# A two-block layer on one core: one group of experts per loop turn, the first expert routed on its own, and one-hot columns as weights in the first four gathers

## The chip, the cores and the metric

One core of one Trainium2 chip runs the whole kernel. The metric is the device time of one execution in microseconds. The kernel before was timed three times: 955.11, 957.72 and 958.09 us, median 957.72 us. The profile is of one further execution.

## The reference, cut to what matters

Two transformer-like blocks over 256 tokens of width 1024, all in float32. The first block is a hybrid mixer (Mamba-2 scan and a short convolution), then a hierarchical mixture of experts; the second block is another mixer and a dense feed-forward. The change touches the start of the kernel, the end of the first mixer and the experts. In the reference:

```python
h = h + hybrid_mixer(rmsnorm(h, norm_mix), ...)
hn = rmsnorm(h, norm_ffn)
h = h + hierarchical_moe(hn, ...)      # 4 groups of 8 experts
# of each token: the best group, the two best experts of that group,
# gates = softmax over groups at the best * softmax over the two logits
# expert e: (silu(x @ w_gate[e]) * (x @ w_up[e])) @ w_down[e]
```

Every expert's three matrices have 2 MB each (1024 x 512 floats), so the 32 experts bring 6 MB each.

## The kernel before, in words

**Memory.** The weights pass through `ring` (six slots of 2 MB), `pair_d` (two more) and three buffers for down matrices, `down_a`, `down_b`, `down_c`. `down_b` lies over `w_hi` and `w_lo`, the split halves of the weights of the first mixer, which are free once its last granule is multiplied. `res` holds the residual stream, 128 partitions (tokens) x 2 blocks x 1024.

**Start.** SP loads x into `x_tok` (L781). ACT and DVE square it, POOL forms the inverse root (`norm_pool`, L505), ACT scales block 1 (L487) and DVE block 0 (L500), PE transposes (`turn_pe`, L515). Meanwhile POOL copies x into `res` with the features reordered (`natural`, L912): in `res` the feature index 8p+c stands at place c*128+p, the order in which the experts' weights lie in memory.

**End of the first mixer.** The last granule of w_out leaves four PSUM banks. `add_res` (L677 to L684) adds them to `res` on DVE, in four pieces with reordered rows. PE transposes the sum for the router (L2200), ACT and DVE copy it out, PE forms the logits (L2209).

**Routing.** A chain of some forty small DVE operations (L1615 to L1675), each waiting for the one before, finds for each token its group and two experts. PE counts ranks (L2216 to L2219) once `member` says that the table of memberships is ready. Between them PE multiplies the identity by itself (`keep_running`, L2040: four and two times 512 columns), results unused. An expert has 32 slots a round; four experts make a group of 128 slots. `gather_first` (L2238) multiplies tokens (as weights, 128x128) by one-hot columns (32 or 96 moving) and so writes the gathered tokens already transposed; `keep_first` and `keep_rest` apply the gain.

**Experts.** `gate_up_apart` (L2251) is the first expert, whose gate matrix is read before its up matrix, so that the gate slot comes free early. `gate_up_pe` and `down_pe` are the others: the 32 gathered tokens are the weights, in four column tiles of the array, and the expert's matrix moves. `add_group` (L2301) scatters a group's results into four PSUM banks that add up over all groups. Groups 0 and 1 are written out; a hardware loop does two groups per turn, three turns here. At the end `add_last` adds the four banks to `res` on DVE (L1783) and PE transposes `res` for the second block (L2314).

**The queue of loads.** SP alone issues the loads of weights, in an order written out by hand (L820 to L868). At the start of the experts these are the last of expert 3 (`pair_d`), the down matrix of expert 1 (`down_b`, L837), then in two halves the gate matrix of expert 4, each behind a half of expert 0's gate product (`gate_read`, L802), then expert 4's up matrix behind expert 0's last product (`gu_raw` 1), expert 5's pair behind `gu_raw` 2, a down matrix behind `ye_raw` 1, and so on. A load behind a wait stops all that stand after it in this queue.

Of the kernel before, what the change touches and what calls it, by code (L numbers as in the profile page):

```python
# [85 lines left out]
def build(nc, ctx, x, w, out):  # L86
# [298 lines left out]
    moe_added = sem("moe_added")  # L385
# [344 lines left out]
    XT_BANK = 7  # L730
    TURN_BANK = ((0, 1, 2, 3, 5, 6, 7, 4), (0, 2, 4, 7, 1, 3, 5, 6), (4, 5, 6, 7, 0, 2, 1, 3))
# [48 lines left out]
    def _(sp):  # L780
        sp.dma_start(x_tok[:, :, :], x.rearrange("(b p) d -> p b d", p=P)).then_inc(ld_x, 16)  # L781
# [54 lines left out]
        load_half(3, 1, 3)  # L836
        load_down(1, 1)  # L837
# [31 lines left out]
        for u in range(UA, len(units)):  # L869
# [13 lines left out]
            if u == UA + SLOTS - 2:  # L883
                sp.wait_ge(const_ready, 6)
# [12 lines left out]
    def _(pool):  # L897
# [13 lines left out]
        for b in range(TB):  # L911
            nc.gpsimd.tensor_copy(natural(b), in_eights(x_tok[:, b, :]))  # L912
# [108 lines left out]
        pool.wait_ge(res_mix, 2)  # L1021
# [28 lines left out]
    def _(act):  # L1050
        load_rows(act, 0)
        act.wait_ge(ld_x, 16)
        norm_act(act, 0, x_tok, xdt)
# [21 lines left out]
        def keep_x(i):  # L1075
            if i == 0:
                act.wait_ge(const_ready, 2)
# [124 lines left out]
        nc.scalar.activation(y_e[:, :], res[:, 0, :], ACT.Square, accum_out=sm[:, 0:1]).then_inc(squared, 1)  # L1202
# [6 lines left out]
        nc.scalar.activation(y_e[:, :], res[:, 1, :], ACT.Square, accum_out=sm[:, 1:2]).then_inc(ss_act, 1)  # L1209
# [28 lines left out]
        group_act(1, 0)  # L1238
        act.wait_ge(routed, 1)
        n_more = act.value_load(rounds_i[0:1, 2:3], min_val=NE // 8 - 1, max_val=NE // 8 * (T // CAP) - 1)  # L1240
        with act.Fori(0, n_more) as i:
            for s in range(2):
                group_act(2 * i + (2 + s), 2 * i + (1 + s))
        keep_left(8 * n_more + 7, 3)

        hi(act, GA)
        hi(act, GA + 1)
# [153 lines left out]
    def _(dve):  # L1401
# [3 lines left out]
        norm_dve(dve, 0, x_tok, xdt)  # L1405
# [186 lines left out]

        def by_token(v, n):
# [19 lines left out]
        for b in range(TB):  # L1613
# [6 lines left out]
        nc.vector.tensor_reduce(g_top, by_group(G_LOGIT), AX_X, ALU.max)  # L1620
# [6 lines left out]
                                                     op0=ALU.mult, op1=ALU.add))  # L1627
        nc.vector.tensor_reduce(g_at, by_group(G_AT), AX_X, ALU.min)
# [26 lines left out]
        dve.wait_ge(rstd_ready, 2)  # L1655
# [877 lines left out]
```

## Time and profile before

| | us |
|---|---|
| three runs | 955.11, 957.72, 958.09 |
| profiled execution | 955.47 |
| its span | 953.7 |

The span is what the profile covers; 1.8 us of the profiled execution lie around it. Busy times and the span in 40 slices of 23.8 us, each digit a busy share in tenths:

```profile
PE 782.6 (82%) x6548; PEld 601.2 (63%) x6548; DVE 465.6 (49%) x815; ACT 318.0 (33%) x525; POOL 99.0 (10%) x116
PE   5999999999984764747646566479999999999997
DVE  6865849547421121201302012024968776766776
PEclk9999999999997887777979798779999999999999
DMA  9895243677999999999999999999975455555101
```

The first ten slices are the first mixer, slices 10 to 28 the experts, the rest the second block. PE leads on the sum, but a sum over stages is not a bound: in the experts' slices the DMA row stands at 9 and PE at 4 to 8, in the mixers it is the other way round. PEclk is the clock granted to TensorE in tenths of full speed.

### The profile page before, as it was taken

The numbers are of one execution on the slowest core, as the hardware profiler recorded it, in microseconds if no ns is written. First come the engines' busy times: TensorE is split into PE (matmuls) and PEld (weight loads), VectorE is DVE, ScalarE is ACT, GpSimd is POOL, SyncE is SP. The second block draws the span as 40 slices with busy tenths as digits, with TensorE's granted clock in tenths as the row PEclk, the third lists the DMA queues.
The fourth block names the chain that finished last, engine by engine and source line by source line (L and its number), as shares of the span: only waits on it lengthen the run. The fifth ranks groups of instructions, "written<-read, shape, count | busy, mean of one in ns | idle before, by whom it ended". The sixth has DMA issues, their size and how long they took to land.

```text
span 953.7 us, 15749 instructions
## 1 busy us (share of the span) xinstructions
PE 782.6 (82%) x6548; PEld 601.2 (63%) x6548; DVE 465.6 (49%) x815; ACT 318.0 (33%) x525; POOL 99.0 (10%) x116
## 2 busy tenths in 40 slices
PE   5999999999984764747646566479999999999997
PEld 5988999777643432334423333236888888888885
DVE  6865849547421121201302012024968776766776
ACT  5764346732100000000000000003597554444444
POOL 3019673300000000000000000000000100000000
PEclk9999999999997887777979798779999999999999
DMA  9895243677999999999999999999975455555101
GB/s 318 272 354 177 90 177 145 259 311 294 415 427 428 426 429 426 427 427 429 428 429 427 428 429 427 429 428 388 363 266 178 155 189 201 183 177 177 45 1 45
DMA packets 72534, 286.67 MB, mean 301 GB/s; under 512 B 11882, under 2 KB 38688, under 8 KB 59936
## 3 DMA queue, kind: packets, MB, share of 16 engines
q1 hardware_dynamic: 71876, 284.81, 75.9%
q10 hardware_dynamic: 604, 1.10, 0.3%
q8 instruction: 39, 0.64, 0.3%
q14 instruction: 15, 0.12, 0.0%
HBM read 284.85 MB, written 1.05 MB: 300 GB/s over the span
## 4 chain that ended last, share of the span: by engine, by line
PE 54%; DMA 28%; issue 8%; DVE 4%; POOL 3%; ACT 2%; SPq 1%; POOLq 0%; DVEq 0%; ACTq 0%
DMA pair_d<-in_w_up_dram 22%; PE bank L664 11%; PE bank L613 11%; PE bank L629 9%; PE bank L2264 5%; PE bank L626 4%; PE bank L2288 4%; PE bank L641 4%; DMA ring<-in_w_in_dram 3%; DMA down_b<-in_w_down_dram 3%; PE bank L2230 1%; PE bank L2238 1%; PE bank L2095 1%; POOL seg_r L946 1%; ACT w_hi L583 1%
## 5 line engine op out<-in xcount | busy, mean ns | idle before, releaser
L593 DVE TENSOR_TENSOR w_lo<-ring,w_hi 128x1024 fp32r<-128x1024 f32 x135 | 174.7, 1294 | 101.9 <-ACT w_hi L583 101.5
L583 ACT ACTIVATE w_hi<-ring 128x1024 fp32r<-128x1024 f32 x136 | 144.2, 1060 | 178.3 <-PE bank L629 64.1
L613 PE MATMUL bank<-act_p,w_hi 128*128 128x256 f32 x736 | 137.7, 288 | 3.1 <-issue 2.0
L1776 DVE COPY y_e<-bank 32x256 f32<-32x256 f32 x64 | 27.2, 424 | 222.5 <-PE bank L2288 222.1
L629 PE MATMUL bank<-act_p,w_hi 128*128 128x512 f32 x344 | 119.3, 397 | 0.0
L613 PEld LDWEIGHTS bank<-act_p,w_hi 128*128 128x128 f32 x736 | 115.3, 192 | 6.0 <-issue 3.9
L1226 ACT ACTIVATE y_e<-bank 32x256 f32<-32x256 f32 x64 | 23.9, 374 | 256.7 <-PE bank L2288 256.4
L613 PE MATMUL bank<-act_p,w_lo 128*128 128x256 f32 x368 | 104.3, 283 | 0.0
L2288 PE MATMUL bank<-down_b,h_t 128*32 128x256 f32 x480 | 40.3, 493 | 74.6 <-issue 64.1
L664 PE MATMUL bank<-w_hi,act_q 128*128 128x512 f32 x288 | 90.6, 396 | 1.4 <-issue 0.8
L2264 PE MATMUL bank<-ring,moe 128*32 128x256 f32 x1472 | 84.0, 380 | 7.1 <-DVE moe L1739 6.7
L626 PE MATMUL bank<-act_p,w_lo 128*128 128x256 f32 x344 | 89.5, 281 | 0.0
L2288 PEld LDWEIGHTS bank<-down_b,h_t 128*32 128x32 f32 x480 | 18.9, 136 | 91.6 <-issue 74.0
L2264 PEld LDWEIGHTS bank<-ring,moe 128*32 128x32 f32 x1472 | 46.9, 110 | 38.6 <-issue 8.6
L629 PEld LDWEIGHTS bank<-act_p,w_hi 128*128 128x128 f32 x344 | 62.5, 188 | 13.1 <-issue 1.2
L613 PEld LDWEIGHTS bank<-act_p,w_lo 128*128 128x128 f32 x368 | 70.7, 192 | 0.0
L2264 PE MATMUL bank<-pair_d,moe 128*32 128x256 f32 x512 | 43.6, 515 | 30.4 <-DMA pair_d<-in_w_up_dram 30.4
L626 PEld LDWEIGHTS bank<-act_p,w_lo 128*128 128x128 f32 x344 | 64.9, 189 | 3.4
L664 PEld LDWEIGHTS bank<-w_hi,act_q 128*128 128x128 f32 x288 | 52.5, 188 | 15.0 <-issue 1.7
L2288 PE MATMUL bank<-down_a,h_t 128*32 128x256 f32 x480 | 37.9, 468 | 25.6 <-DMA down_a<-in_w_down_dram 25.6
L664 PE MATMUL bank<-w_lo,act_q 128*128 128x512 f32 x144 | 56.3, 391 | 0.0
L2264 PEld LDWEIGHTS bank<-pair_d,moe 128*32 128x32 f32 x512 | 24.3, 146 | 49.5 <-issue 46.1
(409 smaller groups left out, 1058.5 us busy)
## 6 DMA issues: line engine op xcount, KB each, us to landing
ring<-in_w_up_dram SPq DMA_DIRECT2D x24, 2048.0 KB, 34.6
ring<-in_w_gate_dram SPq DMA_DIRECT2D x23, 2048.0 KB, 30.2
down_a<-in_w_down_dram SPq DMA_DIRECT2D x15, 2048.0 KB, 25.9
down_b<-in_w_down_dram SPq DMA_DIRECT2D x15, 2048.0 KB, 25.8
ring<-in_w_in_dram SPq DMA_DIRECT2D x14, 2048.0 KB, 17.4
ring<-in_w_ffn_in_dram SPq DMA_DIRECT2D x22, 1024.0 KB, 7.6
pair_d<-in_w_gate_dram SPq DMA_DIRECT2D x8, 2048.0 KB, 30.0
pair_d<-in_w_up_dram SPq DMA_DIRECT2D x8, 2048.0 KB, 34.4
```

The costliest lines, as they stand in the source:

```text
L583: nc.scalar.activation(parts(w_hi, g, view), view, ACT.Copy).then_inc(split_hi, 1)
L593: engine.tensor_tensor(parts(w_lo, g, view), view, h, ALU.subtract).then_inc(split_lo, 1)
L613: mm = nc.tensor.matmul(dst, parts(wt, g, grans[g][1])[:, k, :], a[:, x_part, k, :], start=(k == 0 and i == 0), stop=(k == KC - 1 and i == 2))
L626: mm = nc.tensor.matmul(dst[:, 0:T], parts(w_lo, g, grans[g][1])[:, k, :], a[:, 0, k, :], start=False, stop=False)
L629: mm = nc.tensor.matmul(dst[:, :], parts(w_hi, g, grans[g][1])[:, k, :], a[:, :, k, :], start=(k == 0), stop=(k == KC - 1))
L641: mm = nc.tensor.matmul(dsts[b], a[:, x_part, k0 + k, b * P:(b + 1) * P], parts(wt, g, grans[g][1])[:, k, :], start=(k0 + k == 0 and i == ...
L664: mm = nc.tensor.matmul(banks[2 * b + half][:, :], a_chunk[:, x_part, b * P:(b + 1) * P], wt[:, slot(g), half * 512:(half + 1) * 512], sta ...
L946: ins = nc.gpsimd.tensor_tensor(seg_r[:, n, :, :], bcast(m_le[:, :].unsqueeze(1), [P, 4, P]), bcast(adt_r[:, n, b, 4 * q:4 * q + 4].bitcas ...
L1226: ins = nc.scalar.activation(out_rows(e, j), down_rows(j), ACT.Copy)
L1776: ins = nc.vector.tensor_copy(out_rows(e, j), down_rows(j))
L2264: mm = nc.tensor.matmul(bank[GU_BANK[e % 2]][CAP * j:CAP * (j + 1), 0:2 * P], x_t[:, c, CAP * e:CAP * (e + 1)], gu[:, :, c, j * P:(j + 1) ...
L2288: mm = nc.tensor.matmul(bank[2][CAP * j:CAP * (j + 1), 0:256], h_t[:, e % 2, CAP * c:CAP * (c + 1)], dn[:, c, 256 * j:256 * (j + 1)], star ...
```

## The change

- **Start.** x is loaded straight into `res`, in its own feature order. POOL's two reordering copies (L911, L912) go.
- **End of the first mixer.** `add_res` writes the sum, in plain order, to a new place, `mixed(b)`, which lies in slot 0 of `w_hi` (block 0) and of `w_lo` (block 1), in the memory of `down_b`. PE's router transposes read `mixed` with a step of 8 floats. POOL copies `mixed` in the experts' order to `res` (two copies), and only then builds `m_lt`, the mask that the ranks need. SP's load of `down_b` waits for POOL's copies, the transposes and ACT's squares.
- **First expert alone.** Five small DVE operations decide from the logits whether a token goes to expert 0. Three matmuls with one column each give its rank, and expert 0's one-hot columns are made before the rest of the routing. The gather and the product of expert 0 run while DVE goes on; the full ranks follow on PE behind them.
- **First four gathers.** `gather_alone` takes the one-hot columns as weights (32 wide, in four column tiles) and moves 256 token values through each tile. Its result has slots in partitions, so DVE transposes it in 32x32 blocks and then applies the gain (`keep_alone`). Experts 1, 2 and 3 are gathered one at a time, expert 1 ahead of the others.
- **`keep_running`** multiplies 256 columns, not 512, and stands in other places and counts (3, 2, 2, 1, 6, 2).
- **Residual through PSUM.** In group 0 PE starts each of the four output banks with the identity times `res` (four products of 512 columns). At the end ACT and DVE copy two banks each to `res`; the four DVE adds go.
- **Loop.** Only group 0 is written out; the loop does one group per turn, seven turns.

```diff
+    def mixed(b):
+        at = (2 * b + slot(GA - 2)) * GR
+        return down_b[:, at:at + D]
@@ add_res
-            r = natural(b, 64 * half, 64 * half + 64)
+            cols = slice(half * 512, (half + 1) * 512)
             piece_ready(dve, n, at, g)
-            ins = nc.vector.tensor_tensor(r, r, in_eights(banks[2 * b + half][:, :]), ALU.add)
+            ins = nc.vector.tensor_tensor(mixed(b)[:, cols], res[:, b, cols], banks[2 * b + half][:, :], ALU.add)
@@ sync
-        sp.dma_start(x_tok[:, :, :], x.rearrange("(b p) d -> p b d", p=P)).then_inc(ld_x, 16)
+        sp.dma_start(res[:, :, :], x.rearrange("(b p) d -> p b d", p=P)).then_inc(ld_x, 16)
...
         load_half(3, 1, 3)
+        sp.wait_ge(const_ready, 4)
+        sp.wait_ge(tok_turned, 4)
+        sp.wait_ge(ss_act, 2)
         load_down(1, 1)
         load_first_gate()
@@ gpsimd
         norm_pool(pool, 0)
-        for b in range(TB):
-            nc.gpsimd.tensor_copy(natural(b), in_eights(x_tok[:, b, :]))
...
-        pool.wait_ge(res_mix, 2)
+        for b in range(TB):
+            pool.wait_ge(res_mix, b + 1)
+            ins = nc.gpsimd.tensor_copy(natural(b), in_eights(mixed(b)))
+        ins.then_inc(const_ready, 1)
@@ vector
+        def keep_alone(e):
+            dve.wait_ge(xt_raw, e + 1)
...
+            link_dve(dve, nc.vector.transpose(turned_rows, bank[ALONE_BANK[e]][:, 0:2 * P]))
+            nc.vector.tensor_tensor(x_t[:, :, CAP * e:CAP * (e + 1)], turned_rows.rearrange("p (c s) -> p c s", c=KC),
+                                    bcast(g_ffn[:, :].unsqueeze(2), [P, KC, CAP]), ALU.mult).then_inc(xt_kept, 1)
...
+        nc.vector.tensor_tensor(r8[:, 1, :, :], own, bcast(own[:, :, 0:1], [P, TB, EPG]), ALU.is_gt)
+        link_dve(dve, nc.vector.tensor_reduce(g_top, by_group(G_LOGIT), AX_X, ALU.max))
+        nc.vector.tensor_tensor(r8[:, 2, :, 1], by_group(G_LOGIT)[:, :, 0], g_top, ALU.is_ge)
+        link_dve(dve, nc.vector.tensor_reduce(r8[:, 2, :, 0], r8[:, 1, :, :], AX_X, ALU.add))
+        nc.vector.scalar_tensor_tensor(out=first, ..., op0=ALU.is_le, op1=ALU.mult).then_inc(member, 1)
+        ...                        # rank of expert 0, its one-hot columns: member 2
+        keep_alone(0)              # between two links of the chain
@@ build_group, start
-                keep_first(1)
                 gates()
+                keep_alone(1)
                 rounds()
+                keep_alone(2)
+                keep_alone(3)
                 gate_weights()
@@ tensor
-                                         res[:, b, c * P:(c + 1) * P], ident[:, :])
+                                         in_eights(mixed(b))[:, :, c], ident[:, :])
...
+        nc.tensor.matmul(bank[4][:, 0:1], m_lt[:, :], first[:, 0, :], start=True, stop=True)
+        nc.tensor.matmul(bank[4][:, 1:2], ones[:, :], first[:, 0, :], start=True, stop=False)
+        nc.tensor.matmul(bank[4][:, 1:2], m_lt[:, :], first[:, 1, :], start=False, stop=True).then_inc(rank_raw, 1)
+        keep_running(2)
...
+        def gather_alone(e, which, o):
+            for b in range(TB):
+                row = res[:, b, :].rearrange("t (c p) -> t c p", c=KC)
+                for j in range(4):
+                    mm = nc.tensor.matmul(bank[ALONE_BANK[e]][CAP * j:CAP * (j + 1), 0:2 * P],
+                                          onehot[:, which, b, o:o + CAP], row[:, :, CAP * j:CAP * (j + 1)],
+                                          start=(b == 0), stop=(b == TB - 1))
+            mm.then_inc(xt_raw, 1)
@@ group_pe, before is None
+                gather_alone(0, 1, 0)
+                keep_running(2)
                 gate_up_apart(0)
+                keep_running(1)
+                ranks()
+                keep_running(6)
                 pe.wait_ge(built, 2)
-                gather_first(CAP, P - CAP, bank[5:7], 0)
+                gather_alone(1, 0, CAP)
+                keep_running(2)
+                pe.wait_ge(xt_kept, 2)
+                gate_up_pe(k, 1)
+                for e in range(2, 4):
+                    gather_alone(e, 0, CAP * e)
...
         group_pe(0, None)
-        group_pe(1, 0)
...
-            for s in range(2):
-                group_pe(2 * i + (2 + s), 2 * i + (1 + s))
+            group_pe(i + 1, i)
```

## Rows read from the trace of the kernel before

**Rows 1.** The chain that ended last, in order of time: start us, us, what.
```profile
549.21 34.41 DMA pair_d<-in_w_up_dram
...
636.60 26.40 DMA ring<-in_w_in_dram
```

**Rows 2.** Stretches of the span: busy per engine, then PEclk, DMA share, GB/s.
```profile
229.50:230.00 0.50, 0.50 (x4) 0.26 (x2) 0.34 (x2) 0.00 (x0) 0.00 (x0) 1.00 0.16 66
...
233.00:260.00 27.00, 26.57 (x477) 19.31 (x477) 14.57 (x54) 5.21 (x15) 0.00 (x0) 1.00 0.91 363
260.00:640.00 380.00, 238.14 (x2835) 135.51 (x2834) 74.45 (x204) 27.21 (x80) 0.00 (x0) 0.82 1.01 428
```

**Rows 3.** SP's issues in order of time: start us, us of issuing, engine, line, transfer.
```profile
216.54 0.43 SPq L808 DMA_DIRECT2D down_b<-in_w_down_dram  x1
...
234.65 1.20 SPq L803 DMA_DIRECT2D ring<-in_w_gate_dram  x2
237.26 0.33 SPq L795 DMA_DIRECT2D ring<-in_w_up_dram  x1
...
268.37 0.35 SPq L795 DMA_DIRECT2D ring<-in_w_gate_dram  x1
```

**Rows 4.** The first microseconds in order of time; the last is line L1860's query.
```profile
8.20 4.34 POOL L912 COPY res<-x_tok 128x1024 f32<-128x1024 f32 x2
8.27 2.44 DVE L500 TENSOR_SCALAR xdt<-x_tok,sm 128x1024 f32<-128x1024 f32 x1 [0.83 <-POOL sm L505]
10.79 2.67 DVE L593 TENSOR_TENSOR w_lo<-ring,w_hi 128x1024 fp32r<-128x1024 f32 x1
16.52 1.21 DVE L593 TENSOR_TENSOR w_lo<-ring,w_hi 128x1024 fp32r<-128x1024 f32 x1
L1860 DVE TENSOR_SCALAR res<-nrm,sm x2: 735/738/742, 676.9 to 677.6; 128x1024 f32<-128x1024 f32 x2
```

**Rows 5.** End of the mixer in order of time; the last is line L691's query.
```profile
214.12 3.95 DVE L682 TENSOR_TENSOR res<-res,bank 128x512 f32<-128x512 f32 x4 [1.09 <-PE bank L664]
216.22 1.09 PE L2200 MATMUL bank<-ident,res 128*128 128x128 f32 x8
219.05 3.66 PE L2209 MATMUL bank<-w_rt,moe 128*128 128x36 f32 x32
L691 DVE TENSOR_TENSOR res<-res,bank x4: 686/689/689, 757.6 to 759.7; 128x512 f32<-128x512 f32 x4
```

**Rows 6.** The routing chain in order of time.
```profile
222.75 0.16 DVE L1615 COPY y_e<-bank 128x4 f32<-128x4 f32 x1 [1.38 <-PE bank L2209]
226.64 0.23 DVE L1642 TENSOR_TENSOR y_e<-y_e 128x64 f32<-128x64 f32 x1
227.01 0.38 PE L2216 MATMUL bank<-y_e,gmat 128*128 128x32 f32 x2 [0.79 <-DVE y_e L1642]
227.94 0.16 DVE L1659 COPY y_e<-bank 128x2 f32<-128x2 f32 x1 [0.15 <-PE bank L2219]
229.71 0.17 DVE L1675 SCALAR_TENSOR_TENSOR pos<-y_e 128x4 f32<-128x4 f32 x1
```

**Rows 7.** Filler products, one-hot tables and first experts in order of time.
```profile
222.55 3.68 PE L2040 MATMUL bank<-ident 128*128 128x512 f32 x8
232.10 1.11 DVE L1710 TENSOR_SCALAR moe<-iota_f,pos,sm 128x128 f32<-128x128 f32 x4
233.50 3.70 PE L2251 MATMUL bank<-ring,moe 128*32 128x128 f32 x128
241.60 3.66 PE L2264 MATMUL bank<-ring,moe 128*32 128x256 f32 x64 [0.43 <-DVE moe L1754]
241.86 0.31 DVE L1771 STREAM_TRANSPOSE h_t<-h_m 128x128 f32<-128x128 f32 x1
245.07 1.91 PE L2288 MATMUL bank<-down_a,h_t 128*32 128x256 f32 x32
278.77 3.59 PE L2288 MATMUL bank<-down_b,h_t 128*32 128x256 f32 x32 [2.64 <-issue]
```

More of the change, by code:

```diff
@@ L1237, in _ @@
         group_act(0, None)
[L1238 removed]
         act.wait_ge(routed, 1)
[L1240 removed]
+        n_more = act.value_load(rounds_i[0:1, 2:3], min_val=NE // 4 - 1, max_val=NE // 4 * (T // CAP) - 1)
         with act.Fori(0, n_more) as i:
[L1242 to L1244 removed]
+            group_act(i + 1, i)
+        keep_left(4 * n_more + 3, 3)
         hi(act, GA)
+        for at in range(0, 4, 2):
+            b, half = BY_HALF[at]
+            act.wait_ge(moe_raw, at + 1)
+            nc.scalar.activation(res[:, b, half * 512:(half + 1) * 512], bank[MOE_BANK[at]][:, :], ACT.Copy)\
+              .then_inc(tok_act, 1)
         hi(act, GA + 1)
@@ L1777, in keep_right, with keep_last @@
             ins.then_inc(ye_dve, 1)
-        def add_last():
-            for at, (b, half) in enumerate(BY_HALF):
-                v = res[:, b, half * 512:(half + 1) * 512]
+        def keep_last():
+            for at in range(1, 4, 2):
+                b, half = BY_HALF[at]
                 dve.wait_ge(moe_raw, at + 1)
-                nc.vector.tensor_tensor(v, v, bank[MOE_BANK[at]][:, :], ALU.add).then_inc(moe_added, 1)
+                nc.vector.tensor_copy(res[:, b, half * 512:(half + 1) * 512], bank[MOE_BANK[at]][:, :])\
+                  .then_inc(moe_kept, 1)
         def group_dve(k, before):
@@ L2232, in gather @@
             mm.then_inc(xt_raw, 1)
-        def gather_first(o, n, banks, which):
-            for c in range(KC):
-                for b in range(TB):
-                    mm = nc.tensor.matmul(banks[c // 4][:, (c % 4) * n:(c % 4 + 1) * n], tokens(b, c),
-                                          onehot[:, which, b, o:o + n], start=(b == 0), stop=(b == TB - 1))
-                if c % 4 == 3:
-                    mm.then_inc(xt_raw, 1)
+        def gather_alone(e, which, o):
+            for b in range(TB):
+                row = res[:, b, :].rearrange("t (c p) -> t c p", c=KC)
[4 more added lines that the diff above has]
+            mm.then_inc(xt_raw, 1)
         def gate_up_apart(e):
@@ L2291, in down_pe, with start_output, add_group @@
             mm.then_inc(ye_raw, 1)
-        def add_group(k, first, last):
+        def start_output(at):
+            b, half = BY_HALF[at]
+            nc.tensor.matmul(bank[MOE_BANK[at]][:, :], ident[:, :], res[:, b, half * 512:(half + 1) * 512],
+                             start=True, stop=False)
+        def add_group(k, last):
             pe.wait_ge(ye_act, 4 * k + 4)
@@ L2301, in add_group @@
                 mm = nc.tensor.matmul(bank[MOE_BANK[at]][:, :], gmat[:, b * P:(b + 1) * P],
-                                      y_e[:, half * 512:(half + 1) * 512], start=first, stop=last)
+                                      y_e[:, half * 512:(half + 1) * 512], start=False, stop=last)
                 if last:
@@ L2320, in close_group @@
             down_pe(k, 3)
[L2321 removed]
+            add_group(k, False)
         def group_pe(k, before):
@@ L2336, in group_pe @@
             mm.then_inc(gmat_raw, 1)
-            if before is None:
+            if before is not None:
+                gate_up_pe(k, 1)
+            else:
                 pe.wait_ge(xt_kept, 4)
-            gate_up_pe(k, 1)
             down_pe(k, 0)
@@ L2347, in group_pe @@
             gather(k + 1, 0)
+            if before is None:
+                for at in range(2):
+                    start_output(at)
             down_pe(k, 2)
```

114 lines of the change are left out of this document (53 added, 61 removed).

## The prediction

> **What bounds the kernel now.** I read the 40 slices first, then the chain of waits in order of time, then stretches, and last single instructions where the stretches showed a hole. In the slices the reader sees a DMA row at 9 through the experts. The chain says the same: six times it runs through a transfer into `pair_d` of 32 to 35 us (one of them in the rows), and it leaves the experts through a transfer of 26.40 us that lands at 663.0 [rows 1]. From 260 to 640 us the core loads at 428 GB/s while TensorE works 238 of 380 us and is granted 0.82 of its clock [rows 2]. So in the experts only bytes count, and the length of that stage is bytes over 428 GB/s plus the time in which the queue is dry. A 2 MB matrix takes 4.9 us at this rate.
>
> The queue is dry once, and that is where the change works. It runs empty at 229.5 us (66 GB/s in the half microsecond behind it), and SP issues the next load, the first half of expert 4's gate matrix, only at 234.65, 1.15 us after expert 0's product starts at 233.50 [rows 2, 3, 7]. From 233 to 260 us the mean is 363 GB/s, not 428: 27 x (1 - 363/428) = 4.1 us lost. With the 3.4 us from 229.5 to 233 that makes 7.5 us of lost transfer time, the most that anything between the mixer and the experts can give back.
>
> Outside the experts the chain runs through computing engines from 0 to 229 us, so what is saved early moves everything, the DMA included.
>
> **Start.** POOL's two copies take 4.34 us from 8.20 [rows 4]. DVE's scaling of block 0 stands beside the first and takes 2.44 us; the same form takes 0.738 us elsewhere. The first `w_lo` stands beside the second and takes 2.67 us; the next takes 1.21 us. Both are as long as if they had waited for the copy and then run at their usual length (first copy to about 10.0, plus 0.74, is 10.7; second to 12.2 or so, plus 1.21, is 13.4). The change takes the copies away. PE can then transpose from 9.5, when ACT's half is ready, not from 10.86, and DVE ends its `w_lo` at 12.0, not at 13.4. Both give 1.4 us, and PE is busy without a break behind them. I take 1.4 us, bounds 0.8 and 1.6.
>
> The Trainium skill (SBUF — State Buffer, Who interferes with whom) states that a DVE operation with two SBUF inputs, or in a two-port mode, is fully blocked by a GpSimd operation that holds the shared pair. By that rule the trace agrees, and POOL's copies at their new place block none of `add_res` and the PSUM copies, which have one SBUF input at most.
>
> **End of the mixer.** `add_res` takes 3.95 us for four pieces; in plain order a piece takes 0.689 us [rows 5]. The fourth waits for PE's last product (about 216.2), so the sum is ready at 216.95, not 218.07. PE's transposes took 1.09 us for eight at a time. Their reads get a step of 8 floats, and the trace has no PE read of that kind. Lower bound: nothing. Upper bound: double, 1.1 us for each eight. Nearest rows: DVE took 0.99 us a piece with reordered rows and 0.69 without, a factor of 1.43. I take 0.5 us for each eight. PE then transposes 216.2 to 217.8 and 217.8 to 219.4, and the logits start at 219.4 instead of 219.05: 0.35 us later. At the lower bound they start at 218.4.
>
> The Trainium skill (SBUF — State Buffer, Specifications) has 16-byte cachelines of which a read needs two hits for full speed; a step of 32 bytes hits each line once, which speaks for the upper end. With it the sum below would lose another 1.2 us.
>
> **Expert 0 alone.** From the logits' copy at 222.75 the old chain needs until 226.64 for the memberships, until 227.94 for the rank, and the one-hot columns come 0.7 us after; its gather starts 229.92 [rows 6]. New: logits at 223.1; two links and three unlinked operations at the 0.25 us of a link, 1.15 us: `member` at 224.25. Three matmuls and their copy take what they took (227.01 to 227.94, 0.93 us): 225.3; one-hot columns 0.7 us: 226.0. `gather_alone` has 16 of the 64 instructions of one gate-and-up product [3.66 us, rows 7], 0.92 us plus 0.2 to land: 227.2. `keep_alone` is a transpose of 256 columns (0.31 us for 128, so 0.5) and a product of 256 (0.43, since a table of 128 takes 1.11/4 = 0.28): 228.2. PE starts expert 0 at 228.3 in place of 233.50, 5.2 us earlier. POOL's copies end near 220 (2.2 us each from 215.5), `m_lt` and the root at 221.6: ahead of their use.
>
> SP now issues `down_b` at about 220.2, not at 216.54 [rows 3]. That costs nothing: the two 2 MB loads ahead of it last until 229.5 - 4.9 = 224.6.
>
> First gate half: issued 228.3 + 1.15 = 229.45, flowing 1.0 us later. The queue is dry from 229.5 to 230.45, 0.95 us, and the two halves run up with a loss of 0.5 us (0.8 before). Expert 4's up matrix follows at 232.0, in time. The queue then has work until 230.45 + 0.5 + 9.8 = 240.75.
>
> **Expert 1 is the next hole.** Its load waits for `gu_raw` 2. Before, expert 1 was done at 245.3, and the queue lost 0.7 us there, which is in the 7.5. Now DVE takes up the chain at 228.2: 2.85 us to the memberships (231.05); PE is in expert 0 until 232.0, one filler of 0.46 [256 columns, a half of 3.68/4, rows 7], ranks seen at 233.4; the positions 1.3 us (what lies between 227.94 and 229.88 without the 0.7 that moved); the tables 1.11 and their sum 0.43 [rows 7]: `built` at 236.3. Six fillers on PE take 2.76 and end at 236.6. Gather of expert 1 1.1, `keep_alone` 1.0, product 3.7: 242.5. Its load flows at 243.45, so the queue is dry for 2.7 us. That is what is late next.
>
> Behind it all is covered. Experts 2 and 3 are kept, `gate_weights` and the gated tables follow, and the first down product waits for them until about 249. PE idles some 3.5 us; before, an idle of 2.64 us was followed by a down product of 3.59 us in place of 1.91 [rows 7]. I charge 0.3 us. The starts of the output banks add 4 x 0.92 = 3.7 us to PE in group 0. Expert 8's gate matrix, which waits for PE's expert 4, was issued at 268.37 [rows 3], while what had been issued from 234.65 on, 20 MB (the pairs of experts 4 to 7 and two down matrices), kept the queue busy until 235.6 + 10 x 4.9 = 284.6. The 16 us between take up 7 us of delay.
>
> Lost in all: 0.95 + 0.5 + 2.7 + 0.3 = 4.4 us against 7.5: 3.1 us gained. With free strides 3.8, with doubled transposes 1.9.
>
> **End of the experts and loop.** The DVE adds (0.69 each) become copies on two engines, but ACT's next piece waits for the transfer that lands at 663.0 [rows 1], so this gives nothing; if that cover is gone, 0.5 us. Seven loop turns in place of three: a group's 24 MB take 58.7 us and PE works 238/380 of it, so it has some 20 us of slack per group, and a turn costs nothing until it stalls PE that long.
>
> **Sum.** 1.4 + 3.1 = 4.5 us, so the profiled execution of 955.47 (span 953.7, 1.8 around it) would be 951.0. That execution lies 2.25 us below the median of the three runs, 957.72, from which I forecast 953.2 us.
>
> **Rivals.** *The stride and the second hole eat the gain in the experts.* For it: no row shows such a read, and expert 1's path hands over between DVE and PE many times, each worked out with no slack. Against it: 3.1 us would have to go. With 1.9 us of doubled transposes and 1.5 more for expert 1 it gives 1.4 + 0.4 = 1.8 us: 955.9.
>
> *The filler is too small and the clock falls.* The two filler groups before the first gather drop from 5.5 us to 2.3. If TensorE is granted half its clock when expert 0 starts, expert 0 and 1 take 7.4 us each. `gu_raw` 1 comes at 235.7 (flow 236.7 for a queue empty at 235.35+0.5: 0.8 us), `gu_raw` 2 at 249.9 (flow 250.9, queue empty at 241.6: 9.3 us), and the first down product and expert 2 at half clock let it run dry for another 1.5. Lost: 0.95 + 0.5 + 0.8 + 9.3 + 1.5 = 13.1 us, 5.6 more than before; less 1.4 that is 4.2 us slower, 961.9. It decides from a loss of 8.9 us on, 7.5 + 1.4. For it: the 3.59 us after an idle of 2.64. Against it: in the new order PE's idle stretches before expert 1 are each under 1 us by my sums.
>
> *The gain in the experts isn't there at all*, because transfers issued earlier only wait longer for PE to free the slots behind them. Then the start's 1.4 us remain: 956.3. Against it: the 16 us of backlog at expert 8's issue.
>
> *More than worked out.* Free strides, expert 1 a microsecond earlier, 0.5 at the end: 1.4 + 4.8 + 0.5 = 6.7: 951.0.
>
> **Chances.** Forecast (951.8 to 955) 0.5; stride and second hole 0.17; clock 0.12; no gain in the experts 0.09; more 0.12. Two measurements of this kernel can be told apart from 0.3% on, 2.9 us. The forecast counts as faster in 0.43 of its 0.5, since its own border is near; with 0.12 from the last case and a little from the second this is 0.57. Same: 0.07 + 0.15 + 0.08 = 0.30. Slower: 0.13. The likeliest case alone spans 951.2 to 955.2; the range goes to 949.6 for the fast side and to 957.6 for the two cases with little gain, and leaves out the clock case.
>
> **What would show it.** DVE's scaling of block 0 at about 0.75 us, PE's first transposes at 9.5. The eight router transposes at 1.1 us (free) or 2.2. Expert 0 on PE 5.2 + 1.4 us earlier than 233.5, near 226.9. DMA stretches: a dry place under 1.5 us before expert 4's gate, and one of 2 to 3 us before expert 5's. Group periods of 58.7 us in the loop as before, the transfer that leaves the experts landing 4.5 us earlier, near 658.5, the second block as long as before. I am wrong if PEclk falls under 1.0 before expert 1's product, if the period of a group grows, or if the second dry place is over 5 us.

## The result and the profile after

The changed kernel takes 950.73 us (median of 6 runs, 948.11 to 951.12); the kernel before, on the same chip, 955.98 (954.98 to 958.09). The ratio is 0.9929, 95% interval 0.9919 to 0.9940, which is 5.7 to 7.7 us; the two medians lie 5.3 us apart. The profiled execution took 950.62, span 948.8, beside 955.47 and 953.7. The forecast was 953.2 in a range of 949.6 to 957.6. The direction and the places of the gain were right. The gain was forecast at 4.5 us; it is 5.3 by these medians, 4.85 by the two profiled executions and 5.7 to 7.7 by the interval of the ratio, and it starts from a lower base than the one I forecast from.

Some words for what follows. A hole is a stretch in which the queue of weight loads has little or nothing to move. A filler is a matmul of `keep_running`, whose result nobody uses. A dip is a stretch of some 3 us or more, ahead of the experts' loads at 240 us, in which TensorE's granted clock is 0.50 and not 1.00.

**Start.** The rows that answer to [rows 4], in order of time (start us, us, engine, line):

```profile
8.31 0.75 DVE L500 TENSOR_SCALAR xdt<-res,sm 128x1024 f32<-128x1024 f32 x1 [0.83 <-POOL sm L505]
9.51 3.43 PE L515 MATMUL bank<-ident,xdt 128*128 128x128 f32 x16 [0.75 <-ACT xdt L487]
10.82 1.23 DVE L593 TENSOR_TENSOR w_lo<-ring,w_hi 128x1024 fp32r<-128x1024 f32 x1 [1.76 <-ACT w_hi L583]
```

DVE's scaling fell from 2.44 to 0.75 us, the first `w_lo` from 2.67 to 1.23, and PE starts at 9.51, not 10.86. The mixer runs 1.4 us ahead until 109. The other profiles bear this out: what TensorE does behind its stop near 110 us begins at 110.70 to 111.42 in the eleven profiles with the changed start and at 112.33 to 113.09 in the five with the old one.

**Then the clock.** TensorE stops for 1.8 us, from 109.1 in the changed kernel and from 110.5 in the one before. Behind the stop, the piece of the chain of waits (start us, us, what), first in the kernel before and then in the changed one, and two stretches of the changed one (busy per engine, then PEclk, DMA share, GB/s):

```profile
112.33 3.10 PE bank L613 x24
```
```profile
110.90 4.60 PE bank L613 x24
```
```profile
112.00:114.00 2.00, 2.00 (x11) 2.00 (x11) 1.89 (x6) 0.00 (x0) 0.00 (x0) 0.50 0.03 8
116.00:118.00 2.00, 2.00 (x19) 2.00 (x19) 1.15 (x3) 1.39 (x3) 1.95 (x2) 1.00 0.00 0
```

24 matmuls took 4.60 us at a granted clock of 0.50 (1.2 GHz). In the kernel before they took 3.10 at 1.00. That is 1.5 us, all that the start had saved: the last block of `w_out`'s products begins at 204.81 in this execution and at 204.80 in the one before. From here to expert 0 both mixers stand at the same time.

**End of the mixer and expert 0**, to set beside [rows 5 to 7]:

```profile
216.01 2.10 PE L2213 MATMUL bank<-ident,down_b 128*128 128x128 f32 x16
217.95 3.66 PE L2222 MATMUL bank<-w_rt,moe 128*128 128x36 f32 x32
224.51 1.07 PE L2259 MATMUL bank<-res,moe 128*32 128x256 f32 x16
245.95 0.69 PE L2371 MATMUL bank<-ident,moe 128*128 128x128 f32 x2 [3.67 <-DVE pos L1766]
246.61 3.64 PE L2309 MATMUL bank<-down_a,h_t 128*32 128x256 f32 x32
```

The sixteen router transposes with a step of 8 floats take 2.10 us, 1.05 for eight, where contiguous ones took 1.09: the step is free. The logits start at 217.95 (219.05 before). PE's product of expert 0 begins at 226.78, 6.7 us earlier than before, though the mixer is no earlier.

**The queue.** SP's issues, which answer to [rows 3], and the stretches with a hole:

```profile
219.86 0.33 SPq L814 DMA_DIRECT2D down_b<-in_w_down_dram  x1
227.91 1.20 SPq L809 DMA_DIRECT2D ring<-in_w_gate_dram  x2
240.61 0.33 SPq L801 DMA_DIRECT2D ring<-in_w_gate_dram  x1
250.31 0.33 SPq L814 DMA_DIRECT2D down_a<-in_w_down_dram  x1
```
```profile
229.50:230.50 1.00, 1.00 (x37) 0.80 (x29) 0.52 (x3) 0.00 (x0) 0.00 (x0) 1.00 0.57 213
240.00:244.00 4.00, 2.28 (x44) 1.11 (x36) 2.24 (x9) 0.00 (x0) 0.00 (x0) 1.00 0.72 225
252.00:254.00 2.00, 2.00 (x45) 1.24 (x38) 1.90 (x7) 0.00 (x0) 0.00 (x0) 1.00 0.87 254
229.50:260.00 30.50, 26.83 (x374) 16.79 (x367) 16.02 (x63) 4.09 (x11) 0.00 (x0) 0.89 0.94 371
```

The first hole has shrunk to half a microsecond. The second, ahead of expert 5's matrices, costs 4 x (1 - 225/428) = 1.9 us. A third, which I had not forecast, costs 2 x (1 - 254/428) = 0.8. The load that refills the queue there is a down matrix, issued at 250.31, and it waits for expert 0's down product, which takes 3.64 us at half clock (1.91 before). Expert 2's product ends later still, and SP issues the load behind it at 254.44, when the hole is past. Over 229.5 to 260 the loss is 30.5 x (1 - 371/428) = 4.1 us; before it was 7.4 (324 GB/s). The three holes make 3.2 of the 4.1; the rest lies mainly where the queue starts again behind them (324 GB/s from 230 to 232, 369 from 232 to 234 and from 254 to 256).

**Leaving the experts**, in the chain, beside [rows 1]:

```profile
485.19 34.85 DMA pair_d<-in_w_up_dram
...
544.37 34.43 DMA pair_d<-in_w_up_dram
...
631.75 26.66 DMA ring<-in_w_in_dram
```

The last of these transfers lands at 658.4, 4.6 us earlier than before. By the DMA view the weights' queue moved 21.71 MB from 200 to 260 us where it had moved 20.22 (3.5 us at 428 GB/s), and 76.99 instead of 76.70 MB from 260 to 440 (0.7 us). The second block keeps its length within 0.3 us.

### The profile page after: what moved, and what is told of

It is laid out like the page before. It is cut to its first block, busy times and chain, and to the rows that moved or that the text cites. A ratio compares the mean times of both kernels' runs of the same rounds, so it can differ in the third digit from the quotient of the medians.

```text
span 948.8 us, 15900 instructions
## 1 busy us (share of the span) xinstructions
PE 784.6 (83%) x6582; PEld 601.0 (63%) x6582; DVE 461.6 (49%) x821; ACT 318.4 (34%) x527; POOL 98.0 (10%) x116
## 3 DMA queue, kind: packets, MB, share of 16 engines
HBM read 284.85 MB, written 1.05 MB: 301 GB/s over the span
## 4 chain that ended last, share of the span: by engine, by line
PE 57%; DMA 24%; issue 8%; DVE 4%; POOL 3%; ACT 2%; SPq 1%; POOLq 0%; DVEq 0%; ACTq 0%
DMA pair_d<-in_w_up_dram 18%; PE bank L664 12%; PE bank L613 10%; PE bank L629 9%; PE bank L2285 6%; PE bank L2309 5%; PE bank L626 4%; PE bank L641 4%; DMA ring<-in_w_in_dram 3%; DMA down_b<-in_w_down_dram 3%; PE bank L2250 2%; DVE w_lo L593 1%; PE bank L2108 1%; PE bank L2053 1%; ACT w_hi L583 1%
## 5 line engine op out<-in xcount | busy, mean ns | idle before, releaser
L593 DVE TENSOR_TENSOR w_lo<-ring,w_hi 128x1024 fp32r<-128x1024 f32 x135 | 172.5, 1278 | 103.9 <-ACT w_hi L583 103.5
L2285 PE MATMUL bank<-pair_d,moe 128*32 128x256 f32 x512 | 41.3, 493 | 27.0 <-DMA pair_d<-in_w_up_dram 27.0
L1229 ACT ACTIVATE h_e<-bank 128x128 f32<-128x128 f32 x32 | 8.9, 277 | 134.6 <-PE bank L2285 126.0
```

What stands on the lines that cost most here:

```text
L593: engine.tensor_tensor(parts(w_lo, g, view), view, h, ALU.subtract).then_inc(split_lo, 1)
L2285: mm = nc.tensor.matmul(bank[GU_BANK[e % 2]][CAP * j:CAP * (j + 1), 0:2 * P], x_t[:, c, CAP * e:CAP * (e + 1)], gu[:, :, c, j * P:(j + 1) ...
```

## The experiments

All times are medians; the ratio, with its 95% interval, is to runs of the kernel before on the same chip. The kernel before had 955.98 us beside the result and 956.63, 956.93, 956.52, 956.72 and 957.22 beside the experiments. The interval of a ratio is 1.6 to 3.4 us wide and an experiment has 4 to 12 executions, some with a dip and some without. So a difference of 1 us between two experiments isn't shown by their medians alone. Where it matters I also compare profiles that agree in their dips; each of these is a single execution.

**Does the start count, and what does the clock do to it?**

`e_control`: the changed kernel as it is.

> The changed kernel as it is, as the yardstick for the other three. Both theories: its span 4.9 us below that of the kernel before, 948.8 in its profile; medians some 5 to 7 us apart.

950.88, ratio 0.9937 (0.9923 to 0.9950), as expected; the span of its profile is 948.7. Here the mixer ran at full clock, but behind it:

```profile
220.00:222.00 2.00, 2.00 (x6) 1.64 (x7) 1.07 (x8) 0.00 (x0) 0.00 (x0) 0.50 0.99 426
```

The six fillers behind the logits took 2.71 us in place of 1.37 and the logits 3.73 in place of 3.50, so expert 0 began at 226.75, and nothing of the 1.5 us was left. The dip has moved, and its price with it. A profile of the same TensorE work without any dip comes below, in `e_two_rest`: expert 0 at 225.20, span 947.4, 387 GB/s from 229.5 to 260 us where the control has 369.

`e_pool_back`: POOL's copies at the start again. ACT's first write to `x_tok`, much later, waits for them.

```diff
         norm_pool(pool, 0)
+        for b in range(TB):
+            nc.gpsimd.tensor_copy(x_tok[:, b, :].rearrange("t (c p) -> t p c", c=KC), in_eights(res[:, b, :]))
...
+            if i == 0:
+                act.wait_ge(const_ready, 2)
```

> The changed kernel with POOL's two reordering copies back at the start, from res into x_tok, results unused. Theory A (the start's 1.4 us are real but are lost again when TensorE's clock is halved behind the stop at 109 us): PE's first products at 14.15 again, no half clock at 112 us, and the same time as the control within 0.4 us. Theory B (the 1.4 us count in the result, and the experts gave 3.5): 1.4 us slower than the control.

952.87, ratio 0.9957 (0.9939 to 0.9975), 2.0 us above the control. DVE's two operations are long again (2.43 and 2.12 us). The profile has a dip at 113 and one at 223, and expert 0 begins at 229.67. That is 2.9 us behind the control, which has only the later dip: 1.4 from the start (112.23 against 110.84 behind the stop) and 1.5 from the dip at 113. Theory A falls, since it had no dip here and the time of the control. The time goes with theory B's 1.4 us, but the intervals overlap.

`e_fill_mixer`: three fillers in TensorE's stop at 109.

```diff
+            if g == G_SC + 9:
+                for _ in range(3):
+                    nc.tensor.matmul(bank[c][:, 0:T], ident[:, :], bcast(ident[:, :].unsqueeze(1), [P, 2, P]), start=True, stop=True)
```

> The changed kernel with three products of the identity, 256 columns each, in PE's stop of 1.8 us ahead of granule 29 (109 to 111 us). Theory A (half clock behind an idle stop eats the start's saving): the granted clock stays at 1.00 through 112 to 116 us and the kernel gains 1.4 us over the control. Rival (the saving is lost to something with a fixed time in the mixer, such as the landing of a load): no change, the next stop only grows by 1.4 us.

951.16, ratio 0.9938 (0.9924 to 0.9952): no gain, where theory A had 1.4 us. The clock was 1.00 in the mixer and the dip came at 220, but the control's profile has both as well, so this profile can't say what the fillers do to the clock. The granule (the block of 24 matmuls) behind the stop began 0.4 us later than in the control; the one ahead of the fillers was 0.5 late already.

`e_start_alone`: the kernel before, its two copies moved off the start.

```diff
-        for b in range(TB):
-            nc.gpsimd.tensor_copy(natural(b), in_eights(x_tok[:, b, :]))
...
+        for q in range(4):
+            b, p0 = q // 2, 64 * (q % 2)
+            pool.wait_ge(split_lo, q + 2)
+            nc.gpsimd.tensor_copy(natural(b, p0, p0 + 64), in_eights(x_tok[:, b, 8 * p0:8 * p0 + 512]))
```

> The kernel before, with one part of the change: POOL's two copies no longer stand at the start, they come in four halves behind the split of block 1, where the router's layout is needed only at the end of the mixer. My theory (the start's 1.4 us are real and everything behind them moves with them): in its trace PE's first transposes start at 9.5 and the mixer runs 1.4 us earlier; the queue has then to wait for expert 0 just as long as before, and the time is 1.4 us under the kernel before, 955.2 beside 956.6. Rival (a lowered clock somewhere in the mixer or in front of expert 0 takes it back, as it did in the profiled executions of the changed kernel and of its repetition): the same as the kernel before, 956.6, and a stretch of 3 us at clock 0.50 between 110 and 226 us in its trace.

955.58, ratio 0.9992 (0.9983 to 1.0000): 1.35 us by the medians, 0 to 1.6 by the ratio. Its profile shows neither dip. TensorE's first products begin 1.27 us earlier than before, the block at 26 us 0.82, the granule behind the stop 0.67 (111.66), expert 0 0.66, and the span ends 0.8 earlier. So a lead that is there at 110 us arrives at the end when the clock stays up. `e_loop_alone` shows the same for a delay: with the start of the kernel before it stands 0.76 us behind it at the stop (113.09), 0.76 at expert 0 and 1.0 at the end. It also shows that the 0.67 can't be put down to the edit alone, since four further profiles with the old start lie 0.2 to 0.76 us behind the kernel before at this place.

**Does expert 0's early start count?**

`e_late_first`: its product waits for the full routing, as before the change.

```diff
                 gather_alone(0, 1, 0)
-                keep_running(2)
-                gate_up_apart(0)
-                keep_running(1)
+                keep_running(7)
                 ranks()
                 keep_running(6)
                 pe.wait_ge(built, 2)
+                gate_up_apart(0)
```

> The changed kernel with expert 0's product held back on PE until the full routing is done (its gather stays early). Theory A (what the experts gave is the earlier reload behind expert 0): expert 0 starts at about 233 instead of 226.8, the queue of loads is dry from 229.5 to 235 but no longer before expert 5's pair, and the kernel is 2.5 to 3 us slower than the control. Rival (the gain comes from elsewhere: free strides, residual through PSUM, the loop): at most 1 us slower.

953.03, ratio 0.9974 (0.9960 to 0.9989): 2.2 us above the control by the medians, 3.5 by the ratios. Theory A had 2.5 to 3, the rival at most 1. Expert 0 began at 232.10. The first hole is back and the second is gone, as theory A had it. The rival falls. The queue moved 355 GB/s between 229.5 and 260. This profile has no dip. Beside the one of `e_two_rest`, which has none either, 30.5 x (387 - 355)/428 = 2.3 us of queue time are lost and the span is 2.5 us longer (949.9).

**Are the two holes left worth their length?**

`e_second_apart`: expert 1's product in halves too, and SP's first half load behind the first of them.

```diff
+            if i == 1:
+                sp.wait_ge(gate_read, 3)
+                load_half(i, 0, 4 + i)
...
-                gate_up_pe(k, 1)
+                gate_up_apart(1)
```

> The changed kernel, and expert 1's product is also made in halves of the gate matrix (as expert 0's is), so that SP issues the first half of expert 5's gate matrix when PE has read expert 1's gate matrix, 1.8 us ahead of the end of the product. My theory (the holes in the queue are the experts' whole loss, microsecond for microsecond; the one from 240 to 244 us has 2.2 us): 1.3 to 1.8 us off, 949.1 to 949.6. Rival (the load comes earlier, but the third hole, at 252 to 254 us, which waits for expert 2's product, gets as much longer): 950.9, and as many bytes between 229.5 and 260 as in the changed kernel, 11.3 MB.

949.94, ratio 0.9927 (0.9914 to 0.9941): 0.9 us under the control, less than the 1.3 to 1.8 forecast and not clear of noise. The profile shows why little came of it:

```profile
240.00:244.00 4.00, 1.83 (x36) 0.99 (x27) 2.61 (x10) 0.00 (x0) 0.00 (x0) 1.00 0.98 418
248.00:252.00 4.00, 4.00 (x68) 2.28 (x64) 2.16 (x7) 0.75 (x2) 0.00 (x0) 0.81 0.65 197
```

The second hole is closed, and the third has grown from 0.8 us to 4 x (1 - 197/428) = 2.2, since the load that ends it (issued at 249.78) still waits for expert 0's down product, again at half clock. The load that waits for expert 2's product is issued at 253.24, behind the hole, so it is the down product that counts here and not, as I had put it, expert 2's. That the third hole takes back what the second gives is what the rival said. Without a dip ahead of 240 us the span is 948.2, not under the 947.4 of `e_two_rest`. So the edit alone isn't shown to gain anything.

`e_fill_down`: seven fillers in the wait for the gating tables.

```diff
                 for e in range(2, 4):
                     gather_alone(e, 0, CAP * e)
+                keep_running(7)
```

> The changed kernel with seven further matmuls of no use (3.2 us) in the 3.67 us in which PE waits for the gating tables, before expert 0's down product. In the changed kernel the clock is at half from 244 to 251 us and the down product takes 3.64 us in place of 1.9; expert 2's product then ends at 254.4, and the queue has 1.0 us less to do at 252 to 254. My theory: the clock stays at its upper level, expert 2's product ends 1.5 us or more earlier, the hole at 252 to 254 goes, and the time falls by 0.9 us, to 950.0. Rival (that idle stretch is covered by the queue, as I had put it, and costs nothing): 950.9, with the hole still there for another reason.

950.13, ratio 0.9929 (0.9916 to 0.9942), 0.75 us under the control, near the 0.9 forecast but inside the noise of the medians. What the profile shows is plain: the down product takes 1.93 us and the third hole is gone, at full clock:

```profile
252.00:254.00 2.00, 2.00 (x44) 1.43 (x38) 1.90 (x8) 0.28 (x1) 0.00 (x0) 1.00 0.98 410
```

`e_best`: both, and the ranks between the halves of expert 0's product. The fillers change with it: one ahead of the ranks and two behind the product in place of one and six.

```diff
                 mm.then_inc(gu_raw if n else gate_read, 1)
+                if (e, n) == (0, 0):
+                    keep_running(1)
+                    ranks()
...
-                keep_running(1)
-                ranks()
-                keep_running(6)
+                keep_running(2)
```

> The changed kernel with three additions: expert 1's product in halves of the gate matrix, TensorE's ranks for all experts between the two halves of expert 0's product (about 1.4 us earlier), and seven matmuls of no use in TensorE's wait for the gating tables. My theory (holes in the queue count one for one): the second hole, 2.2 us, is closed by 1.8 + 1.4 us, the third, 0.9 us, goes with the clock: 950.9 - 3.1 = 947.8. Rival (the parts overlap: the two earlier runs gave 1.0 and 0.8 us, and the rest of the loss is the change from one load to the next with halves): 949.1.

947.75, ratio 0.9914 (0.9901 to 0.9928), faster than both kernels: 3.1 us under the control by the medians, as my theory had it, 2.2 by the ratios. That it hit 3.1 is in part luck, since the control's profile has a dip and this one has none. Beside `e_two_rest`, without a dip too, the span is 2.5 us shorter (944.9). From 229.5 to 260 the queue now loses 30.5 x (1 - 411/428) = 1.2 us, where `e_two_rest` loses 2.9 and the control 4.2:

```profile
229.50:260.00 30.50, 29.14 (x490) 20.99 (x484) 16.68 (x62) 4.74 (x13) 0.00 (x0) 1.00 1.00 411
```

**The loop.**

`e_two_per_turn`: two groups a turn in the changed kernel, as before the change.

```diff
-            group_pe(i + 1, i)
+            for s in range(2):
+                group_pe(2 * i + (2 + s), 2 * i + (1 + s))
```

(and the same for ACT and DVE, with a second group ahead of the loop)

> The changed kernel with only the loop undone: two groups of four experts a turn, three turns, and two groups ahead of it, as in the kernel before. My theory (the form of the loop is worth nothing): 950.9, as the changed kernel. Rival (the turns with two groups fetch more instructions over the same DMA engines and cost part of a microsecond; the kernel before had 39 instruction packets and 0.64 MB, the changed one 32 and 0.52 MB, and the second group's period was 59.3 us in place of 58.7): 951.4, 39 packets again, and a first group period in the loop of 59.2 to 59.3.

955.73, ratio 0.9990 (0.9979 to 1.0002): 4.9 us, far more than either theory had. Nearly the whole gain of the change is gone.

`e_loop_alone`: the opposite edit in the kernel before, with two groups still written out ahead of the loop.

> The kernel before with only the loop changed: one group of four experts a turn (six turns), two groups still ahead of it. The forecast had this at nothing. Undoing the same edit in the changed kernel cost 4 to 5 us and 25 more instruction packets, and its group periods grew from 58.7 to 59.4 to 59.8 us. Theory L (the turns with two groups make an engine fetch its instructions again on the weights' DMA engines, in the kernel before as well, in its first turn and in many executions later on): 0.5 to 1.5 us under the kernel before, no instruction packets between 380 and 630 us, periods of 58.7. Rival N (the kernel before fetches once and no more; only the changed kernel's bodies are too long for it): 0 to 0.5 us.

956.49, ratio 1.0001 (0.9993 to 1.0010): nothing, as rival N allowed. `e_two_pe` and `e_two_rest` split the undone loop by engine:

> The changed kernel with two groups a turn on TensorE alone; ScalarE and VectorE keep one group a turn. TensorE has by far the most instructions in a group. Theory P (TensorE's longer body is what is fetched again and again): 955, over 50 instruction packets, periods of 59.4 to 59.8, as with all three engines. Rival Q (another engine's body, or all three together): 951, 32 to 36 packets, periods of 58.7.

> The changed kernel with two groups a turn on ScalarE and VectorE, and one on TensorE: the counterpart. Theory P: 951, 32 to 36 instruction packets, periods of 58.7. Rival Q: 955, over 50 packets.

955.39 (ratio 0.9987, 0.9977 to 0.9997) and 950.00 (0.9937, 0.9920 to 0.9953): it is TensorE's loop (theory P). The DMA queue that brings instructions, over the whole span (packets, MB, share), in the changed kernel:

```profile
q8 instruction: 32, 0.52, 0.2%
```

and with TensorE's two groups a turn, over the span and from 440 to 520 us:

```profile
q8 instruction: 57, 0.93, 0.4%
q8 instruction: 5, 0.08, 0.4%
```

In the kernel before and in the changed one there is none from 440 to 630 us. Yet the kernel before has the same body on TensorE, 428 matmuls; only 1799 stand ahead of it and not 1816. So I moved it:

```diff
             pe.wait_ge(gmat_kept, k + 1)
+            if isinstance(k, int) and k == 1:
+                for _ in range(17):
+                    nc.tensor.matmul(bank[XT_BANK][:, 0:8], ident[:, :], ident[:, 0:8], start=True, stop=True)
             gather(k + 1, 0)
```

> The kernel before (two groups a turn) with 17 matmuls of 8 columns and no use added on TensorE in group 1, ahead of the loop, where TensorE waits some 10 us for weights. Its instruction stream then has as many matmuls ahead of the loop (1816) as the changed kernel with TensorE's loop undone, and the same body (428 matmuls, 456 instructions). Theory W (where the body begins in the stream decides whether its instructions are fetched again each turn): over 50 instruction packets, periods of 59.4 to 59.8, and 2 to 5 us slower than the kernel before. Rival V (something else in the changed kernel brings the fetches): 39 or 40 packets, the time of the kernel before.

> The same with 64 such matmuls (1863 ahead of the loop). Theory W leaves two cases: by the remainder of the position (39 packets and the time of before are then possible again), or by a limit that lies between 1799 and 1816 (over 50 packets, 2 to 5 us slower). Rival V: the time of the kernel before.

> The changed kernel with two groups a turn on TensorE and 47 such matmuls in group 1, so that its loop too begins behind 1863 matmuls. Theory W: as many packets in the loop as the kernel before with 64, whichever that is; if those are none, the time comes back to 951 from 955.4. Rival V: 955.4 and over 50 packets whatever the other shows.

> The kernel before with 32 matmuls of no use in group 1, ahead of the loop. In the trace each such matmul has two TensorE rows and two weight loads, so 64 of them are 256 instructions, and an instruction packet has 16 KB. Theory R (the loop's body, some 1,730 TensorE instructions, touches one more packet's worth of code at some places than at others, and the place repeats every 64 matmuls): 32 is the far side of that period, so over 50 packets, and 1.5 to 5 us slower than the kernel before. Rival A (the address must be a round one, and 32 is as round as 64): 39 to 41 packets, the time of the kernel before.

| kernel | matmuls ahead | packets | us | ratio to before |
|---|---|---|---|---|
| before, 17 more | 1816 | 57 | 959.60 | 1.0036 (1.0023 to 1.0049) |
| before, 32 more | 1831 | 57 | 959.47 | 1.0027 (1.0013 to 1.0040) |
| before, 64 more | 1863 | 40 | 956.97 | 1.0002 (0.9993 to 1.0011) |
| changed, two groups on PE, 47 more | 1863 | 40 | 951.29 | 0.9955 (0.9940 to 0.9971) |

In the first two rows the kernel before is beside its own runs, 956.72 and 957.22; 17 and 32 more matmuls cost 2.9 and 2.3 us. The last row is to be set beside the 955.39 of `e_two_pe`: 47 more matmuls, and it is 4.1 us faster. Theory W (the place of the loop decides) holds in both kernels. Theory R (the place repeats every 64 matmuls) agrees with all four places tried, and no others were tried. SP's issues of the same matrix, one a group, with 17 more (a row between left out):

```profile
435.25 0.38 SPq L795 DMA_DIRECT2D pair_d<-in_w_up_dram  x1
...
554.47 0.38 SPq L795 DMA_DIRECT2D pair_d<-in_w_up_dram  x1
```

and with 64:

```profile
432.10 0.38 SPq L795 DMA_DIRECT2D pair_d<-in_w_up_dram  x1
...
549.59 0.38 SPq L795 DMA_DIRECT2D pair_d<-in_w_up_dram  x1
```

Two periods take 119.2 us with 17 more and 117.5 with 64.

## Why the prediction was off, step by step

- **From the profile to the median: the step that failed.** The sum gave 951.0 for the profiled execution, and 950.62 came. Then I added the 2.25 us by which 957.72 stood above the profile of before, to 953.2. That difference belonged to three runs. Later medians of the kernel before are 955.98 to 957.22, that is 0.5 to 1.75 above its profile, and the changed kernel's medians lie 0.1 and 0.4 above its two profiles. Beside the 955.98 measured with the result, 953.2 is a gain of 2.8 us, about half of the 5.3 that came. In part the profile of before is itself an early one: of the five with the old start it is the first to pass the stop at 110 us, by 0.2 to 0.76.
- **The gain itself was put too low as well**, 4.5 us where the ratio has 5.7 to 7.7. The terms that were mis-sized are the step of 8 floats, the loop and the path of expert 1, below.
- **That the profile hit the sum is luck.** The forecast had 1.4 from the start and 3.1 from the experts' first loads. In this profile the dip left nothing of the 1.4. The loads to 260 us gave 3.5, those from 260 to 440 gave 0.7, and some 0.7 more came behind, 0.4 to the last transfer and 0.3 in the second block. The forecast had nothing for what came behind 260 us.
- **Start, 1.4 us.** The saving is there (9.51, and 1.4 us ahead at 109). In the profile shown, the clock took it back. The forecast had a lowered clock only as an all-or-nothing rival at expert 0; what comes is a small dip, 1.5 us, at 112 or at 220, in some executions. `e_two_rest`, which does TensorE's work of the changed kernel, had neither dip: its span is 947.4, 1.4 under the changed kernel's 948.8 and 6.3 under before.
- **Step of 8 floats.** Taken at 0.5 us for eight, measured 0: the logits came at 217.95 with the mixer no earlier, where I had 219.4 and my lower bound was 218.4. By my own alternative free strides are worth 0.7 us. The Trainium skill (SBUF — State Buffer, Specifications) would have had such reads slow; for PE's transposes the trace contradicts it, 1.05 us with the step beside 1.09 without.
- **POOL and DVE.** The Trainium skill (SBUF — State Buffer, Who interferes with whom) is borne out: with POOL's copies gone the two DVE operations have their usual length, and in `e_pool_back` they are long again.
- **Expert 0.** Forecast from the logits' start to PE's product 228.3 - 219.4 = 8.9 us; measured 226.78 - 217.95 = 8.8. The first hole, with its restart, costs 1.3 us beside 0.95 + 0.5 forecast.
- **Expert 1.** Forecast 14.2 us behind expert 0's start; its end came at 240.6, 13.8 behind. The hole costs 1.9 us with its restart, beside 2.7 forecast.
- **The idle before the first down product.** Forecast 3.5 us of idle and a charge of 0.3; there were 3.67 us, and 0.8 us lost at 252 to 254. `e_fill_down` closes that hole; its median is 0.75 lower. I had the half clock in a row [rows 7] and followed it as far as the down product, but not to the load that waits for this product.
- **The loop, forecast nothing.** For a turn that is right. But the kernel before fetched code for the copy of group 1 ahead of the loop and then for the body, 10 packets from 260 to 440 us beside 4 after; its period ending at 407.55 was 59.27 us, beside 58.73 in the changed kernel. `e_loop_alone` keeps that copy and gains nothing (59.26). So the change probably gains some 0.5 us here; no run changes that copy alone. The larger part is what it avoided: with two groups a turn the same change is worth 1.2 us of the medians, not 5 to 6. That loss was not in the forecast as a rival, and that the change escaped it is luck, for I had put the loop at nothing.
- **What sums up.** Without dips 1.4 + 3.8 (free strides) + 0.5 (loop) = 5.7, and `e_two_rest` shows 6.3 between spans; with one dip of 1.5 it would be 4.2, and the two profiles show 4.85 and 5.0. Of the 0.6 to 0.8 between, 0.4 may be expert 1's earlier end; the rest stays open. Both dip-free and dipped figures are of one or two executions.
- The rival "no gain in the experts" falls by `e_late_first` and `e_best`; "stride and second hole" by the transposes and by the second hole's 1.9 us. The residual through PSUM was not tested by itself: from the last transfer of the experts to the end only 0.3 us changed.

## What to carry over

Forecast the change of a profile and add it to several medians of the old kernel, not to one of three runs. Where one queue is the bound, list its dry places, go from each to the instruction whose end releases the next load, and count the sum of all of them, not one alone: closing the second hole by itself made the third one longer (`e_second_apart`), while `e_best` took the loss from 2.9 us to 1.2 and the span down by 2.5. When two profiles are compared, see first that both have the same dips; one is worth 1.5 us here. With a loop body as long as this one, look at the instruction packets inside the loop before and after every edit, even of one far ahead of it.

## What the chip showed that was not expected

- **A loop's place in the code can cost 2.3 to 4.1 us.** In the kernel before, the same body of 428 matmuls had no instruction packet from 440 to 630 us behind 1799 and 1863 matmuls; behind 1816 and 1831 it had 6 and 5 from 440 to 520 and 8 from 520 to 630. The changed kernel with two groups on TensorE had 5 and 9 behind 1816 and none behind 1863. A packet has 0.93/57 = 0.0163 MB. The trace shows two matmuls and two weight loads for each of the added ones (x128 for 64), so 64 are 256 instructions. The Trainium skill (Advanced Engine Details and Errata, ISA Cache) gives a cache line of 16 KB for 256 instructions, which agrees with both the size and the repeat at 64. How many lines TensorE holds isn't shown by these runs. Nor is why 17 packets (57 against 40) cost that much, when their 0.28 MB are 0.65 us at 428 GB/s; that each holds up one of the DMA engines on which a load is spread is argued only.
- **The granted clock falls at places that change from run to run.** Ahead of 240 us the 18 profiles show it at 0.50 near 112 (behind the stop of 1.8 us) in one, near 220 (TensorE busy without a stop from 200 on, last with logits and fillers) in three, at both in two (`e_pool_back`, `e_shift17`) and nowhere in twelve, among them the kernel before and `e_best`. The changed kernel as it is had it at 112 in one profile and at 220 in the other. What decides it stays open.
